# Expert down products as three one-pass products, with low weight parts by GpSimd and down weights issued by the sync queue

## The reference, cut to what matters

```python
for e in range(N_EXPERTS):
    act = jax.nn.silu(hf @ w_gate[e]) * (hf @ w_up[e])
    out = out + combine[:, e:e + 1] * (act @ w_down[e])
```

## Time and profile before

| | |
|---|---|
| time, median of three executions | 2214.78 us (2211.32 to 2216.1) |
| time of the profiled execution | 2210.18 us, span of its profile 2208.6 us |
| PE busy | 2121.1 us, 96% |
| DVE busy | 1212.5 us, 55% |
| ACT busy | 951.9 us, 43% |
| POOL busy | 185.7 us, 8% |
| chain that ended last | PE 85%, DVE 7%, ACT 4%, DMA 2% |

### The profile page before, as it was taken

The page is one execution under the profiler, slowest core; times in us unless marked ns, Lnnn a source line. Parts: engine busy times, 40 slices in busy tenths (PEclk is TensorE's granted clock), DMA queues, the critical chain, the costliest instruction groups (busy, mean ns, idle before and its releaser), DMA issues.

```text
span 2208.6 us, 25770 instructions
## 1 busy us (share of the span) xinstructions
PE 2121.1 (96%) x9980; PEld 1660.3 (75%) x9980; DVE 1212.5 (55%) x1830; ACT 951.9 (43%) x1484; POOL 185.7 (8%) x235
## 2 busy tenths in 40 slices
PE   7999999999999968999999999999999999999998
PEld 4768678877776637887778888878877767888887
DVE  6747654478777745367544454463446646445444
ACT  4455532346655524236431134343357755112343
POOL 1240001101000010000000000020223200000000
PEclk9999999999999988999999999999989999999999
DMA  9304034939999972220222222232100012222221
GB/s 396 118 27 178 7 127 162 380 129 362 383 382 383 384 266 92 93 88 18 77 96 102 98 95 96 96 106 96 64 2 2 3 50 91 101 102 93 100 96 58
DMA packets 55345, 309.31 MB, mean 140 GB/s; under 512 B 10830, under 2 KB 11603, under 8 KB 24117
## 3 DMA queue, kind: packets, MB, share of 16 engines
q1 hardware_dynamic: 36788, 230.25, 28.2%
q0 software_dynamic: 11520, 41.60, 4.8%
q10 hardware_dynamic: 6916, 35.81, 4.6%
HBM read 276.24 MB, written 30.99 MB: 139 GB/s over the span
## 4 chain that ended last, share of the span: by engine, by line
PE 85%; DVE 7%; ACT 4%; DMA 2%; issue 1%; POOL 0%; ACTq 0%; DVEq 0%; POOLq 0%
PE PB L1727 62%; PE PB L2244 5%; PE PB L2502 3%; DMA BIG<-in_k_caus 1%; PE PB L2476 1%; PE PB L2475 1%; PE PB L2436 1%; PE PB L1879 1%; PE PB L1900 1%; DVE WL L2641 1%; PE PB L2002 1%; PE PB L2073 1%; PE PB L2509 1%; PE PB L2192 1%; DVE X L2699 1%
## 5 line engine op out<-in xcount | busy, mean ns | idle before, releaser
L2641 DVE TENSOR_TENSOR WL<-RING,WH 128x1024 fp32r<-128x1024 f32 x228 | 281.8, 1236 | 595.4 <-ACT WH L972 386.1
L972 ACT CAST WH<-RING 128x1024 fp32r<-128x1024 f32 x228 | 239.4, 1050 | 770.1 <-PE PB L1727 764.9
L1727 PE MATMUL PB<-HTH,WH 128*128 128x512 f32 x1056 | 412.8, 391 | 5.4 <-DVE HTL L2668 3.7
L1727 PE MATMUL PB<-HTL,WH 128*128 128x512 f32 x1056 | 411.5, 390 | 0.0
L1727 PE MATMUL PB<-HTH,WL 128*128 128x512 f32 x1056 | 411.4, 390 | 0.0
L1727 PEld LDWEIGHTS PB<-HTH,WH 128*128 128x128 f32 x1056 | 198.6, 188 | 49.0 <-issue 6.1
L1727 PEld LDWEIGHTS PB<-HTH,WL 128*128 128x128 f32 x1056 | 198.6, 188 | 41.8
L1727 PEld LDWEIGHTS PB<-HTL,WH 128*128 128x128 f32 x1056 | 198.7, 188 | 40.8
L1727 PE MATMUL PB<-WH,NHH 128*128 128x512 f32 x496 | 193.2, 390 | 1.8 <-DVE NHL L2646 1.8
L1727 PE MATMUL PB<-WH,NHL 128*128 128x512 f32 x496 | 193.0, 389 | 0.0
L1727 PE MATMUL PB<-WL,NHH 128*128 128x512 f32 x496 | 193.0, 389 | 0.0
(11 more groups left out here) (589 smaller groups left out, 3419.7 us busy)
## 6 DMA issues: line engine op xcount, KB each, us to landing
RING<-in_mlp_w_packed SPq DMA_DIRECT2D x64, 1024.0 KB, 4.8
RING<-in_expert_w_gate_packed SPq DMA_DIRECT2D x32, 1024.0 KB, 7.4
RING<-in_expert_w_up_packed SPq DMA_DIRECT2D x32, 1024.0 KB, 11.3
BIG<-in_expert_w_down_packed ACTq DMA_DIRECT2D x30, 1024.0 KB
RING<-in_w_in_packed SPq DMA_DIRECT2D x20, 1024.0 KB, 5.0
BIG<-in_ada_packed SPq DMA_DIRECT2D x9, 2048.0 KB, 9.4
dispatch_rows<-BIG POOLq DMA_DIRECT2D x24, 512.0 KB, 18.8
RING<-in_a_w_in_packed SPq DMA_DIRECT2D x10, 1024.0 KB, 5.0
```

What stands on the lines that cost most here:

```text
L972: ins = nc.scalar.copy(split_weights(stage, q)[0], halves_of(n, q))
L1727: yield pe.matmul(dst, lhs, rhs, start=(start and n == 0), stop=(stop_ and n == 2))
L2641: return V.tensor_tensor(wl, halves_of(n, q), wh.bitcast(F32), ALU.subtract)
```

## The change

The down products become three one-pass products. ACT writes the high part of each half of the down weights (`down_high`, 128x2048, into `DNH`), POOL its low part (`DNL`), and then SP, not ACT, issues the load of the next expert's half into `DNW` (`next_down_weights`). The activations get a high part on ACT (`act_high`) and a low part on DVE (`product_low`, in the place of `product_T`). The last expert's down weights go through the ring, and DVE writes their low parts (`last_down_low`). The load of the final gain row moves to the last iteration.

```diff
+            def next_down_weights(e, m):
+
+                sp.wait_ge(dn_lo, down_low_no(e - 1, m))
+                sp.dma_start(DNW[:, m], tall(a["expert_w_down_packed"][e], 0, m * W)).then_inc(expert_down_in[m], 16)
+
             for e in range(EXPERTS):
                 for m in range(4):
+                    if m in (1, 2) and 2 < e:
+                        next_down_weights(e - 2, m - 1)
                     expert(GU_AT[e] + m, a["expert_w_gate_packed"] if m < 2 else a["expert_w_up_packed"], e, KK * (m % 2), 0)
             for half in range(2):
+                next_down_weights(EXPERTS - 2, half)
                 expert(LAST_DOWN + half, a["expert_w_down_packed"], EXPERTS - 1, 0, half * W)
...
+            def down_high(e, m):
+
+                if e == EXPERTS - 1:
+                    n = CH["moe"] + LAST_DOWN + m
+                    act.wait_ge(arrived[n % SLOTS], slot_count(n))
+                    act.wait_ge(part_begun, part_no("moe", 8 * e + 4 + 2 * m) + 1)
+                else:
+                    act.wait_ge(expert_down_in[m], DOWN_IN0[m] + 16 * (e + 1))
+                    if e > 0:
+                        act.wait_ge(down_done, 2 * (e - 1) + m + 1)
+                nc.scalar.copy(down_parts(e, m)[0], down_raw(e, m)).then_inc(dn_hi, 1)
...
             for e in range(EXPERTS):
+                if e > 0:
+                    down_high(e - 1, 0)
                 expert_high(e, 5)
-                if 1 < e < EXPERTS:
-                    act.wait_ge(down_done, 2 * (e - 1) - 1)
-                    expert_down_weights(e - 1, 0)
-                    act.wait_ge(down_done, 2 * (e - 1))
-                    expert_down_weights(e - 1, 1)
                 expert_high(e, 6)
+                if e > 0:
+                    down_high(e - 1, 1)
                 expert_high(e, 7)
+                if e > 0:
+                    act_high(e - 1)
                 if e + 1 < EXPERTS:
                     expert_high(e + 1, 0)
...
-            for e in range(EXPERTS):
-                if e > 0:
-                    rows_in(e + 1, (e + 1) % 2, 2, disp[(e + 1) * P:(e + 2) * P, :])
+            rows_in(2, 0, 2, disp[2 * P:3 * P, :])
+            for e in range(1, EXPERTS):
+                for m in range(2):
+                    high, low = down_parts(e - 1, m)
+                    pool.wait_ge(dn_hi, down_high_no(e - 1, m))
+                    nc.gpsimd.tensor_tensor(low, down_raw(e - 1, m), high.bitcast(F32), ALU.subtract).then_inc(dn_lo, 1)
+                if e + 2 <= EXPERTS:
+                    rows_in(e + 2, e % 2, 2, disp[(e + 2) * P:(e + 3) * P, :])
                 if e > 1:
                     rows_out(e - 2, e % 2, back[(e - 2) * P:(e - 1) * P, :])
...
+            def expert_down(e, between=None):
+
+                pe.wait_ge(a_ht, e + 1)
+                pe.wait_ge(y_ev, e + 1)
                 for m in range(2):
                     if between is not None and m == 1:
                         between()
-                    w = weights(m)
+                    pe.wait_ge(dn_lo, down_low_no(e, m))
                     for k in range(KK):
-                        ins = pe.matmul(PB[5 + m][:, :], ACTT[e % 2][:, k, :], w[:, k, :], start=(k == 0), stop=(k == KK - 1))
-                        if k == 0 and starts:
-                            begin(ins, None)
+                        for n, ins in enumerate(three(PB[5 + m][:, :], down_parts(e, m), k, act_parts(e), k, "N", slice(0, P),
+                                                      k == 0, k == KK - 1)):
...
                 if e > 0:
-                    product_T(e - 1, (e - 1) % 2)
+                    product_low(e - 1)
...
+                else:
+                    for m in range(2):
+                        last_down_low(m)
                 product(e, e % 2)
```

More of the change, by code:

```diff
@@ L302, in program @@
     x_rows = sem("X_rows_updated")
-    fg_dve, fg_act = sem("forget_vector"), sem("forget_scalar")
+    fg_dve, fg_act = sem("forget_vector"), sem("forget_then_expert_parts_by_scalar")
     f_rows_in, f_pads = sem("forget_rows_in"), sem("pads_cleared")
     heads_high, heads_low = sem("head_operands_high"), sem("head_operands_low")
-    fq_ready = sem("fox_q_ready")
+    fq_ready = sem("fox_q_then_expert_low_parts_by_pool")
     fm_done, fm_max, fmt_done, fm_row = (sem(f"fox_max_{x}") for x in ("products", "reduced", "transposed", "row"))
@@ L326, in program @@
     half_merged = sem("half_merged")
+    dn_hi, dn_lo = fg_act, fq_ready
     x_hi, x_lo = sem("moe_rows_high"), sem("moe_rows_low")
@@ L376, in program @@
     RWS, RWSUM, RW = big(14336, ND, 20), BIG[:, 14496:14516], big(14528, ND, 20)
-    FINAL_ROW = QS[:, :, :].rearrange("p a b -> p (a b)")
+    FINAL_ROW = nc.alloc_sbuf_tensor_at("FINALR", [P, D], F32, offset=htl_at + 4 * 4 * T)[:, :]
     DNW = big(12288, 2, KK, W)
@@ L381, in program, with down_high_no, act_high_no, down_low_no @@
     HIT1 = PT[:, 0, :, :]
+    assert wl_at == wh_at + 4 * 2 * 2 * W
+    DNH = nc.alloc_sbuf_tensor_at("DNH", [P, 2, KK, W], F32R, offset=wh_at)
+    DNL = nc.alloc_sbuf_tensor_at("DNL", [P, 2, KK, W], F32R, offset=score_at)
+    ACTH, ACTL = (nc.alloc_sbuf_tensor_at(n_, [P, 4, P], F32R, offset=nat_at + 4 * (D + i * DFF)) for i, n_ in
+                  enumerate(("ACTH", "ACTL")))
+    LACTH, LACTL = (nc.alloc_sbuf_tensor_at(n_, [P, 4, P], F32R, offset=htl_at + 4 * i * DFF) for i, n_ in
+                    enumerate(("LACTH", "LACTL")))
+    def down_high_no(e, m):
+        return 2 + 3 * e + m + 1
+    def act_high_no(e):
+        return 2 + 3 * e + 3
+    def down_low_no(e, m):
+        return NH1 + 2 * e + m + 1
+    def down_raw(e, m):
+        n = CH["moe"] + LAST_DOWN + m
+        return slot(n) if e == EXPERTS - 1 else DNW[:, m]
+    def down_parts(e, m):
+        if e == EXPERTS - 1:
+            at_ = (8 * e + 2 + 2 * m) % MOE_SLOTS
+            return tuple(t[:, at_:at_ + 2].rearrange("p s k n -> p (s k) n") for t in (EWH, EWL))
+        return DNH[:, m], DNL[:, m]
+    def act_parts(e):
+        return tuple(t[:, :, :] for t in ((LACTH, LACTL) if e == EXPERTS - 1 else (ACTH, ACTL)))
     def rows_banks(E):
@@ L1249, in _, with act_high @@
             expert_rows_high(0)
+            def down_high(e, m):
+                if e == EXPERTS - 1:
+                    n = CH["moe"] + LAST_DOWN + m
+                    act.wait_ge(arrived[n % SLOTS], slot_count(n))
[5 more added lines that the diff above has]
+                nc.scalar.copy(down_parts(e, m)[0], down_raw(e, m)).then_inc(dn_hi, 1)
+            def act_high(e):
+                act.wait_ge(a_tp, e + 1)
+                nc.scalar.copy(act_parts(e)[0].rearrange("p a b -> p (a b)"), PB[4][:, :]).then_inc(dn_hi, 1)
             for e in range(EXPERTS):
+                if e > 0:
+                    down_high(e - 1, 0)
                 expert_high(e, 5)
-                if 1 < e < EXPERTS:
-                    act.wait_ge(down_done, 2 * (e - 1) - 1)
-                    expert_down_weights(e - 1, 0)
-                    act.wait_ge(down_done, 2 * (e - 1))
-                    expert_down_weights(e - 1, 1)
                 expert_high(e, 6)
+                if e > 0:
+                    down_high(e - 1, 1)
                 expert_high(e, 7)
+                if e > 0:
+                    act_high(e - 1)
                 if e + 1 < EXPERTS:
@@ L1268, in _ @@
                         expert_high(e + 1, j)
+                else:
+                    act.wait_ge(gu_done, e)
+                    act.dma_start(FINAL_ROW, row_on_all(a["final_g"])).then_inc(row_in, 16)
+                    for m in range(2):
+                        down_high(e, m)
                 if e == 0:
@@ L1273, in _ @@
                     expert_high(e + 1, 4)
+            act_high(EXPERTS - 1)
             act.wait_ge(routed, 3)
@@ L2233, in act_T, with down @@
                 ins.then_inc(a_tp, 1)
-            def down(E, e, weights, starts, between=None):
+            def down(E, e, weights):
                 pe.wait_ge(a_ht, E + 1)
@@ L2239, in down @@
                 for m in range(2):
-                    if between is not None and m == 1:
-                        between()
                     w = weights(m)
@@ L2244, in down @@
                         ins = pe.matmul(PB[5 + m][:, :], ACTT[e % 2][:, k, :], w[:, k, :], start=(k == 0), stop=(k == KK - 1))
-                        if k == 0 and starts:
-                            begin(ins, None)
                     ins.then_inc(down_done, 1)
             def expert_down(e, between=None):
[L2251 to L2258, removed]
+                pe.wait_ge(a_ht, e + 1)
+                pe.wait_ge(y_ev, e + 1)
+                for m in range(2):
+                    if between is not None and m == 1:
+                        between()
+                    pe.wait_ge(dn_lo, down_low_no(e, m))
+                    for k in range(KK):
```

(19 more changed lines are left out.)

2 lines of the change are left out of this document (removed).

## The result

The changed kernel takes 2347.15 us (median of four executions, 2342.74 to 2349.8), the kernel before 2214.85. The ratio is 1.0598, 95% interval 1.0577 to 1.0619: 132 us slower, where 2347 us was forecast.

A forecast was written before the change was run, and what follows sets the result against it. PE was taken to bound the expert loop. Losses of 5 + 122 + 5 = +132 us on the profiled 2210.18 give 2342, and 4.6 to the median gives 2347 us; range 2262 to 2385, the case's own 2330 to 2370.

The forecast's parts named there:

- The gain on PE: Down products in the expert loop: 24 one-pass products take 5.47 us for 6.87, 1.40 us less an expert, 17.7 us an iteration.
- The exclusion: In the loop, DVE low parts (10.4 us) and POOL subtractions (9.2 us) cannot overlap, 19.6 us together; alone +79 us, 6%.
- The walk: Hand-timed loop of loads, ACT, POOL, DVE and PE, from low part 3 to the next: 28.5 us an iteration.
- The plain sum 14.1 + 9.2 = 23.3: DVE's and POOL's work in one iteration simply added; with 1.05 us for the rows' high part, 24.4 us.
- The late halves: Down-weight loads queued behind chunks: half 0 lands 7.4 us after issue, 3 us too late; alone about +50 us, 12%.
- The turn by hand: One loop iteration timed step by step: 28.5 us, 9.4 more than before.
- the prediction's allowance for the speed of the transfers: Down-weight loads at 2.5 or 2.8 us per MiB: half 1 0.4 earlier or 0.8 later, total loss 127 to 142 us.
- The 13 middle turns: Iterations 2 to 14 of the expert loop lose 9.4 us each, 122 us.
- The first: Iteration 1, its down weights already loaded, loses only to the exclusion: 24.4 us, 5.3 more.
- The last: Last expert, with its two low parts on DVE and half 1 as late: some 5 us.
- The clock: Rival: PE idling ahead of part 5 lowers its clock; hidden if brief, +228 us if it stays, 2443 us; 9%.

The follow-up runs named there:

- e6: Kernel of e3 with each load of down weights after the first pair halved to 0.5 MiB: 2197.09 us, ratio 0.9912.
- e1: Changed kernel with POOL's two subtractions an iteration replaced by memsets of about the same time that read nothing: 2273.56 us, ratio 1.0269.
- e2: Changed kernel with both halves of the next down weights issued ahead of chunk 0 in the sync queue: 2283.95 us, ratio 1.0303.
- e9: Kernel of e2 with POOL's subtraction of half 1 made twice: 2360.81 us in one execution.
- e5: Changed kernel with down-weight low parts by DVE, none on POOL, and both halves issued ahead of chunk 0: 2231.66 us, ratio 1.0070.
- e3: Changed kernel with memsets for POOL's subtractions and both halves issued ahead of chunk 0: 2204.63 us, ratio 0.9953.

## Why the prediction was right

**The gain on PE.** 1.40 us an expert, 17.7 us a turn: e6 shows 17.74. Right, and worth nothing while other engines bound the loop.

**The exclusion.** It rested on one overlap in the trace of before, and was the step with most weight on least evidence. e1 against the changed kernel settles it (74 us). The walk had it right: two blocked low parts a turn, 4.71 and 4.37 us, and DVE stands still for 6.7 us of POOL's 9.2 in that turn, 104 us in all (255.8 - 151.9 on the two pages). The plain sum 14.1 + 9.2 = 23.3, on which the expectation of e2 is built, is not shown by e2's turns of 22.9 to 23.9: there too DVE lost 6.7 us and idled for 3.0, and the agreement in number is partly luck. That a further subtraction is paid almost in full is what e9 shows (4.35 us).

**The late halves.** The hand counts from the issue of the chunk ahead of each half. Half 0 landed 7.3 us after chunk 0's issue (719.25 - 711.94; 7.4 by hand), half 1 10.0 us after chunk 1's (724.22 - 714.22; 10.3 by hand). e2 gives back 63 us.

**The turn by hand.** 28.5 us against 28.36 on average, and the steps fit, not only their sum. From chunk 1's issue at 714.22, low part 5 is written after 12.65 us (12.9 by hand), POOL's second subtraction ends after 17.1 (17.5), low part 7 is written after 19.3 (19.8) and low part 3 after 28.1 (28.5). In the walk as in the chain the loop closes over half 0 and low part 1: half 1's cast is done 0.75 us before low part 5 (0.6 by hand), and POOL waits for that low part. So the prediction's allowance for the speed of the transfers, 127 to 142 us, is taken from the wrong half: by its own walk half 1 has 0.6 us to spare, half 0 would move by 0.2 or 0.4 us, and the allowance is 129 to 137. In the trace POOL's second subtraction begins 0.67 us before low part 5 is written and reads 5.09 us, not 4.6. PE idled less than in the walk, 4.3 and 3.5 us for 6.6 and 4.4, since part of its work ran at the low clock.

**The terms of the sum.** The 13 middle turns were put at 122 us and cost 121.1. The first was put at 5.3 on the wrong base: it does take 22.5 us (24.4 by hand), but before it took 13.0, not 19.1, since it has no down products; it lost 9.5. The last was put at 5 and lost 2.4 up to its `silu`; from there to the end of its down products it was 1.7 us shorter than before (13.5 for 15.2). The errors are 4.2 and -4.3, and the 2.5 us lost ahead of the first `silu` are in no term, so part of the closeness of 2347 to 2347.15 is luck.

**The clock.** The rival held in its first half only. The granted clock does fall in each turn, and comes back some 10 to 14 us later, in two of the nine turns between 550 and 800 us with a return to 0.98 or more in between (from:to us, us, then the columns as above):

```profile
726.00:728.00 2.00, 1.07 (x5) 0.90 (x6) 2.00 (x4) 2.00 (x4) 1.80 (x1) 1.00 0.26 37
728.00:730.00 2.00, 0.94 (x3) 0.21 (x1) 2.00 (x2) 1.91 (x5) 2.00 (x1) 0.51 0.78 295
...
736.00:738.00 2.00, 2.00 (x6) 1.61 (x5) 0.89 (x3) 1.45 (x2) 0.00 (x0) 0.50 1.04 434
738.00:740.00 2.00, 2.00 (x9) 1.59 (x9) 2.00 (x3) 2.00 (x3) 0.00 (x0) 0.93 0.18 74
```

PE had no product between about 722.7 and 726.9. From 728 to 738 it then worked at 1.2 GHz, and had the time: it is not in the chain of this turn. In a turn later PE is in the chain from 761.10 for 14.66 us, the first four or so at the low clock, and four of the turns are 0.5 to 1.2 us longer than the others' 28.0 to 28.3; that the clock makes that difference is likely and not shown, since no run held the clock up.

**What was not foreseen** is in e5: the place for half 0 that was early enough in a turn of 23 us was too late in one of 19.

## What to carry to other kernels

Before work is moved from VectorE to an idle GpSimd, add up what both read from SBUF: VectorE operations with two SBUF operands and GpSimd operations that read SBUF exclude each other, so what of their times meets adds up. Here VectorE stood still for 6.7 of the 9.2 us that GpSimd worked in a turn, and those 9.2 us on an engine that was 8% busy cost more than 4.6 us on one that was 74% busy in the loop. The Trainium skill (Perfetto Trace Analysis, Optimizing Scalar/DVE Operations) warns that such a move might not help; here the exclusion cost 74 us.

A transfer that moves to another queue takes on the waits of all that stand ahead of it. Write down when its data are wanted and when the wait in front of it is met; an issue early enough in a long turn must be checked again for the short one.

Even an engine-bound loop can sit next to its transfer bound: this one moved 384 GB/s before the change, would have needed 414 at PE's new pace, and reached 407 in e3, so PE's 22 us were not all to be had. Read the bound from the bytes and from a run with fewer of them; the DMA share was 0.97 in e6 too, where PE set the pace.

## What the runs showed of the hardware that I had not expected

- The exclusion alternates. When both engines have work that contends, neither starves: one GpSimd subtraction (4.55 us), one VectorE low part, the next GpSimd one (in e9 for three subtractions in a row). A subtraction that waits inside counts the wait as its own duration: 5.39 to 5.53 us in e9, 5.09 in the changed kernel.
- GpSimd memsets, which only write, leave VectorE's low parts at 1.22 us (e1).
- The transfers sustained 407 GB/s at a share of 1.01 over 180 us of e3's loop. The same stretch before:

```profile
580.00:760.00 180.00, 180.00 (x717) 124.85 (x716) 133.55 (x162) 106.34 (x136) 9.61 (x18) 1.00 0.99 384
```

  So a share of 0.99 was not yet the end: 6% more bytes a microsecond went through. And e6 shows 0.97 with 355 GB/s. Why the share stays so high with fewer bytes was not tried.
- PE's granted clock came back in each turn, 10 to 14 us after it fell, although PE was idle for several us twice in every turn.
